# Two-block transformer kernel: one group of memory values and one modulation row change places, and token-major groups wait chunk by chunk

## The reference

```python
# first block, for each of 2 layers
h = layer_norm(ALPHA * h + 0.5 * swiglu(h, ffn1_gate[l], ffn1_up[l], ffn1_down[l]), ...)
z = h @ w_in[l]                      # split into the inputs of three mixers
mix = concat([y_conv, y_rec, y_pool]) @ w_out[l]
h = layer_norm(ALPHA * h + mix, ...)
h = layer_norm(ALPHA * h + cross_attn(h, mem, ca_q[l], ca_k[l], ca_v[l], ca_o[l]), ...)
h = layer_norm(ALPHA * h + 0.5 * swiglu(h, ffn2_gate[l], ffn2_up[l], ffn2_down[l]), ...)

def cross_attn(x, mem, wq, wk, wv, wo):   # 4 heads of 256
    q, k, v = x @ wq, mem @ wk, mem @ wv  # 256 memory rows
    ... softmax(q k^T) v, then @ wo

# second block: attention and an expert layer in each of 2 layers,
# shifted and scaled by rows that depend on a condition c alone
mod = silu(c) @ ada_w[i] + ada_b[i]       # 6 x 1024 per layer; the same for c_ctx
w = softmax(top scores) * gelu(u_tab[expert] . h)   # 128 rows gathered per token
out = sum over the 128 of w * v_tab[expert]
```

## Time and profile before

| | us |
|---|---|
| timed runs, median of 3 (lowest, highest) | 3248.68 (3248.24, 3252.84) |
| the profiled execution, device time | 3234.46 |
| its span from first to last instruction | 3232.2 |
| TensorE busy | 3055.6 (95%) |
| VectorE busy | 2133.4 (66%) |
| ScalarE busy | 952.0 (29%) |
| GpSimd busy | 1226.2 (38%) |

### The profile page before, as it was taken

One profiled execution on the slowest core, in us unless ns is written; L12 is line 12 of the kernel. 1 busy time (PEld: TensorE's weight loads), 2 busy tenths in 40 slices (PEclk: granted clock), 3 DMA queues, 4 the chain that ended last, 5 costly groups with the idle time before them and its releaser, 6 DMA issues.

```text
span 3232.2 us, 39640 instructions
## 1 busy us (share of the span) xinstructions
PE 3055.6 (95%) x13179; PEld 2183.1 (68%) x13185; DVE 2133.4 (66%) x4328; ACT 952.0 (29%) x2504; POOL 1226.2 (38%) x1136
## 2 busy tenths in 40 slices
PE   9999999999999999999999999989888999987777
PEld 7688888888888888887885845535335855532224
DVE  7877889756555457766455695667555596577444
ACT  2320012211001002121003464335455464343333
POOL 1003545344435443343430254434443144444332
PEclk9999999999999999999999999999999999999999
DMA  9787989798998997788988899999999899999998
GB/s 363 256 288 281 373 352 350 267 359 330 355 353 347 356 330 272 268 338 344 354 308 294 336 422 419 421 419 421 418 421 378 319 420 420 421 421 421 421 421 352
DMA packets 252469, 1164.47 MB, mean 360 GB/s; under 512 B 27304, under 2 KB 34952, under 8 KB 186400
## 3 DMA queue, kind: packets, MB, share of 16 engines
q0 software_dynamic: 153792, 828.44, 63.6%
q1 hardware_dynamic: 98480, 334.10, 28.5%
q10 hardware_dynamic: 48, 0.05, 0.0%
HBM read 1161.39 MB, written 1.10 MB: 360 GB/s over the span
## 4 chain that ended last, share of the span: by engine, by line
PE 32%; DMA 16%; DVE 5%; ACT 4%; issue 1%; POOL 0%; ACTq 0%; SPq 0%; POOLq 0%; DVEq 0%
DMA ring<-in_peer_uv,idx 12%; PE ps_a L1471 12%; PE ps_b L1529 5%; DMA arena<-in_peer_uv,idx 3%; PE ps_a L1537 2%; DVE ring L2962 2%; ACT arena L1762 2%; PE ps_a L774 1%; PE ps_b L1292 1%; PE ps_b L1237 1%; PE ps_b L787 1%; ACT L1762 1%; PE ps_a L1292 1%; PE ps_b L1028 1%; ACT wts L1762 1%
## 5 line engine op out<-in xcount | busy, mean ns | idle before, releaser
L1471 PE MATMUL ps_a<-ring,arena 128*128 128x512 f32 x1728 | 819.4, 608 | 129.1 <-ACT arena L1762 128.6
L749 POOL DMA_INDIRECT ring<-in_peer_uv,idx x448 | 494.8, 1104 | 879.0 <-PE ps_a L1471 620.8
L2962 DVE SCALAR_TENSOR_TENSOR ring<-ring,h_tm 128x1024 f32<-128x1024 f32 x448 | 546.7, 1223 | 378.0 <-DMA ring<-in_peer_uv,idx 377.3
L712 POOL DMA_INDIRECT ring<-in_peer_uv,idx_now x512 | 580.7, 1134 | 415.3 <-DVE arena L2780 151.4
L1471 PEld LDWEIGHTS ps_a<-ring,arena 128*128 128x128 f32 x1728 | 308.1, 191 | 561.3 <-ACT arena L1762 293.8
L1529 PE MATMUL ps_b<-x_t,ring 128*128 128x256 f32 x2816 | 623.3, 380 | 0.8 <-DMA ring<-in_ffn 0.5
L1529 PEld LDWEIGHTS ps_b<-x_t,ring 128*128 128x128 f32 x2816 | 533.6, 190 | 79.0 <-ACT x_t L1762 3.5
L1762 ACT ACTIVATE arena<-ps_b 128x256 f32<-128x256 f32 (+3 forms) x218 | 99.3, 457 | 1195.9 <-PE ps_b L1529 827.7
L1537 PE MATMUL ps_a<-arena,ring 128*128 128x256 f32 x1408 | 318.7, 380 | 0.0
L2780 DVE SCALAR_TENSOR_TENSOR arena<-ring,h_tm 128x1024 f32<-128x1024 f32 x256 | 299.1, 1220 | 20.0 <-DMA ring<-in_peer_uv,idx_now 16.6
L1537 PEld LDWEIGHTS ps_a<-arena,ring 128*128 128x128 f32 x1408 | 267.7, 190 | 39.1 <-issue 3.5
(11 more groups left out here) (460 smaller groups left out, 3357.9 us busy)
## 6 DMA issues: line engine op xcount, KB each, us to landing
ring<-in_ffn SPq DMA_DIRECT2D x264, 512.0 KB, 7.0
wring<-in_second_w SPq DMA_DIRECT2D x166, 512.0 KB, 4.8
wring<-in_mix_w SPq DMA_DIRECT2D x120, 512.0 KB, 6.4
ring<-in_ada_rows POOLq DMA_DIRECT2D x44, 512.0 KB, 5.7
ring<-in_second_w SPq DMA_DIRECT2D x12, 1024.0 KB, 10.2
ring<-in_peer_uv,idx_now POOLq DMA_INDIRECT x512, 8.4
ring<-in_peer_uv,idx POOLq DMA_INDIRECT x448, 14.8
arena<-in_second_w SPq DMA_DIRECT2D x13, 512.0 KB, 11.1
```

What stands on the lines that cost most here:

```text
L712: G.indirect_dma_start(rows[:, s, :], None, table, bass.IndirectOffsetOnAxis(ap=idx_now[:, half, s:s + 1], axis=0)).then_inc(rows_in[s], p ...
L749: G.indirect_dma_start(pairs[slot].rearrange("p c d -> p (c d)"), None, a["peer_uv"], bass.IndirectOffsetOnAxis(ap=idx[:, b, s:s + 1], axi ...
L1471: ins = mm(ps_a[:, b * D + j * 512:b * D + (j + 1) * 512], diags[:, at % DIAGS, :], pairs[at % PAIRS][:, 1, j * 512:(j + 1) * 512], start= ...
L2962: V.scalar_tensor_tensor(row, row, 1.0, h_tm[:, n // SLOTS, :], ALU.mult, ALU.mult, accum_out=dots[:, n % SLOTS:n % SLOTS + 1]).then_inc(d ...
```

## The change

Three things.

1. Layer 1's group 13 (chunks 26 and 27 of its `mix_w`, `MOVED` = 26) leaves the mixer. It is computed in layer 0's last norm by `moved_between` into `ps_b[:, 512:1024]` and copied by ScalarE to `moved_v`. The chunks behind it are loaded and counted without it; the groups' banks alternate accordingly.
2. The modulation row that stood in that norm goes to VectorE, as a second row in layer 1's first feed-forward: `mod_row_sums(1, 0, row_acc_2, 1)` behind the first eight slots. TensorE sums it over partitions into `ps_c`, ahead of the other row's product, and ScalarE takes it from there first. SyncE loads this row at the start of the stage, into slots 2, 3, 0, 1; the row that was loaded there is now loaded between the fourth and the fifth turn of the loop. Because of the shifted slots, `value_between` uses slots 2 and 3 in layer 1.
3. `tm_group` runs the chunks outside, over both token blocks, and waits for each chunk when it comes to it; `last_values` also waits for each chunk by itself.

```diff
@@ SyncE
                     if w == 0:
-                        mod_row_loads(row_at)
+                        mod_row_loads(row_at - l, 2 * l)
...
-                    with sp.loop(FT_TURNS, **ff_turn) as i:
+                    looped = FT_TURNS - 1 if (l, w) == (1, 0) else FT_TURNS
+                    with sp.loop(looped, **ff_turn) as i:
...
-                    if w == 0:
+                    if (l, w) == (0, 0):
                         chunk_loads(a["mix_w"], mix_at, MIX_CHUNKS - WR)
+                    elif (l, w) == (1, 0):
+                        mod_row_loads(row_at, 2)
+                        for ft in range(FT_STEP):
+                            for part in range(3):
+                                ff_loads(looped * FT_STEP + (l * (2 * FT) + (w * FT + 2 + ft)), ft, part)
+                        chunk_loads(a["mix_w"], mix_at, 2, 2)
+                        chunk_loads(a["mix_w"], mix_at + 2, MOVED - 2)
+                        chunk_loads(a["mix_w"], mix_at + MOVED + 2, MIX_CHUNKS - WR - MOVED - 2)
+                    elif l == 0:
+                        chunk_loads(a["mix_w"], MIX_CHUNKS + MOVED, 2)
                     else:
                         mod_row_loads(row_at + 3)
@@ TensorE
             def tm_group(c, bank, src):
-                w = [chunk((c + t) % WR) for t in range(2)]
-                for b in range(NB):
-                    for k in range(KT):
-                        ins = mm(bank[:, b * T:(b + 1) * T], src[:, k, b * P:(b + 1) * P],
-                                 w[k // 4][:, (k % 4) * T:(k % 4 + 1) * T], start=k == 0, stop=k == KT - 1)
-                        if b == NB - 1 and k in (3, 7):
-                            ins.then_inc(chunk_done, pe.adds(chunk_done))
+                for t in range(2):
+                    w = chunk((c + t) % WR)
+                    for b in range(NB):
+                        for k in range(4 * t, 4 * t + 4):
+                            ins = mm(bank[:, b * T:(b + 1) * T], src[:, k, b * P:(b + 1) * P],
+                                     w[:, (k % 4) * T:(k % 4 + 1) * T], start=b + k == 0, stop=k == KT - 1,
+                                     skip_group_check=True)
+                    ins.then_inc(chunk_done, pe.adds(chunk_done))
...
                 gate_up(0, True)
                 mod_row_free()
+                if second_row:
+                    eng.wait_ge(z_done, pe.now(z_done))
...
                 eng.wait_ge(chunk_done, pe.now(chunk_done))
+                if second_row:
+                    mm(ps_c[0:2, :], mean_d[:, 0:2], row_acc_2, start=True, stop=True).then_inc(
+                        row_summed, pe.adds(row_summed))
+                    pe.skip(mod_row_taken, 1)
...
                 between(0, 1)
+                if between == value_between and l:
+                    eng.wait_ge(mod_row_taken, pe.now(mod_row_taken, 1))
...
+            def moved_between(i0, i1):
+                if i0 == 0:
+                    mod_row_free()
+                for i in range(i0, i1):
+                    b, k = i // KT, i % KT
                     if b == 0 and k % 4 == 0:
                         chunk(k // 4)
-                    ins = mm(ps_b[:, b * T:(b + 1) * T], mem_t[:, k, b * P:(b + 1) * P],
+                    ins = mm(ps_b[:, 512 + b * T:512 + (b + 1) * T], mem_t[:, k, b * P:(b + 1) * P],
                              wring[:, k // 4, (k % 4) * T:(k % 4 + 1) * T], start=k == 0, stop=k == KT - 1)
...
-                group(13, 26, mem_t, tm=True)
+                if l == 0:
+                    group(13, MOVED, mem_t, tm=True)
...
-                layer_norm(mod_row_between, finish if l == L - 1 else None)
+                layer_norm(mod_row_between if l else moved_between, finish if l == L - 1 else None)
@@ ScalarE
                 feed_forward()
+                if l:
+                    mod_row_take(row_at - 1, SECOND_ROW, mod_row)
                 mod_row_take(row_at, 2, mod_row)
...
-                mod_row_take(row_at + 3, 1, mod_row)
+                if l == 0:
+                    eng.wait_ge(chunk_done, ac.next(chunk_done, 2))
+                    act(moved_v, ps_b[:, 512:1024].rearrange("p (b t) -> p b t", t=T), ACT.Copy).then_inc(
+                        z_done, ac.adds(z_done))
+                else:
+                    mod_row_take(row_at + 3, 1, mod_row)
@@ VectorE
                 hidden_tile(0)
                 some_slots(summing, h, at, HEAD_SLOTS, acc_first)
+                if (l, w) == (1, 0):
+                    mod_row_sums(l, w, row_acc_2, 1)
                 with ve.loop(FT_TURNS, up_done=FT_STEP, silu_done=FT_STEP, down_done=FT_STEP, hidden_done=FT_STEP,
                              **per_turn) as i:
```

More of the change, by code:

```diff
@@ L540, in _, with mod_row_loads @@
             chunk_loads(a["early_w"], 6, 2, 2)
-            def mod_row_loads(i):
-                chunk_loads(a["second_w"], LAYER_1 + WR * ROW_AT[i], WR)
+            def mod_row_loads(i, first=0):
+                chunk_loads(a["second_w"], LAYER_1 + WR * ROW_AT[i], WR, first)
             chunk_loads(a["second_w"], FIRST_ADA, QKV_CHUNKS)
@@ L1589, in value_between @@
                     b, k = i // KT, i % KT
+                    s = k // 4 + 2 * l
+                    if b == 0 and k % 4 == 0:
+                        chunk(s)
+                    ins = mm(ps_b[:, b * T:(b + 1) * T], mem_t[:, k, b * P:(b + 1) * P],
+                             wring[:, s, (k % 4) * T:(k % 4 + 1) * T], start=k == 0, stop=k == KT - 1)
+                    if b == NB - 1 and k % 4 == 3:
+                        ins.then_inc(chunk_done, pe.adds(chunk_done))
+                if i1 == 2 * KT:
+                    pe.skip(z_done, 1)
+            def moved_between(i0, i1):
[3 more added lines that the diff above has]
+                    b, k = i // KT, i % KT
                     if b == 0 and k % 4 == 0:
                         chunk(k // 4)
-                    ins = mm(ps_b[:, b * T:(b + 1) * T], mem_t[:, k, b * P:(b + 1) * P],
+                    ins = mm(ps_b[:, 512 + b * T:512 + (b + 1) * T], mem_t[:, k, b * P:(b + 1) * P],
                              wring[:, k // 4, (k % 4) * T:(k % 4 + 1) * T], start=k == 0, stop=k == KT - 1)
@@ L1623, in group @@
                     eng.wait_ge(z_done, pe.now(z_done, 1))
-                    odd = (g + 1 if g < 12 else g) % 2
+                    odd = (g + 1 if g < 12 or l and g < 18 else g) % 2
                     bank = ps_b[:, odd * 512:(odd + 1) * 512]
+                    if l and c < MOVED:
+                        c += 2
                     if tm:
@@ L1792, in mod_row_take @@
             def mod_row_take(i, bank, row):
-                if bank == 2:
+                if bank in (2, SECOND_ROW):
                     eng.wait_ge(row_summed, ac.next(row_summed))
@@ L2328, in _ @@
                 group(11, z_g[:, 2:4, :], ACT.Sigmoid)
-                group(13, ca_v[:, 1])
+                if l == 0:
+                    group(13, ca_v[:, 1])
                 eng.wait_ge(o_done, ac.next(o_done))
@@ L3166, in later_search, with mod_row_sums @@
                     expert_ids(0, 1, 4, split=True)
-            def mod_row_sums(l, w):
-                loads = ROW_LOADS + l * (MIX_CHUNKS // WR + 4) + w * (MIX_CHUNKS // WR + 2)
+            def mod_row_sums(l, w, row=row_acc, back=0):
+                loads = ROW_LOADS + l * (MIX_CHUNKS // WR + 4) + w * (MIX_CHUNKS // WR + 2) - back
+                first = 2 if (l, w) == (1, 0) else 0
                 for k in range(KT):
-                    part, weight = wring[:, k // 2, k % 2 * 512:(k % 2 + 1) * 512], cond[:, 2 * k:2 * k + 1]
+                    s = (first + k // 2) % WR
+                    part, weight = wring[:, s, k % 2 * 512:(k % 2 + 1) * 512], cond[:, 2 * k:2 * k + 1]
                     if k % 2 == 0:
-                        eng.wait_ge(weights_in[k // 2], 16 * loads)
+                        eng.wait_ge(weights_in[s], 16 * (loads + 1 if s < first else loads))
                     if k == 0:
-                        ins = V.tensor_scalar(row_acc, part, weight, None, ALU.mult)
+                        ins = V.tensor_scalar(row, part, weight, None, ALU.mult)
                     else:
                         eng.wait_ge(row_step, ve.now(row_step))
-                        ins = V.scalar_tensor_tensor(row_acc, part, weight, row_acc, ALU.mult, ALU.add)
+                        ins = V.scalar_tensor_tensor(row, part, weight, row, ALU.mult, ALU.add)
                     if k < KT - 1:
```

39 lines of the change are left out of this document (26 added, 13 removed).

## The result

The changed kernel takes 3256.62 us, the median of 14 runs (3253.44 to 3260.22), the kernel before beside it 3249.89 us (14 runs, 3245.61 to 3252.84). The ratio is 1.0019, 95% interval [1.0012, 1.0027]: 6.7 us slower by the medians. The forecast was 3250.4 us, 1.7 us slower, in a range of 3242 to 3256; the time lies 0.6 us above it.

A forecast was written before the change was run, and what follows sets the result against it. The prediction took TensorE to bound the changed stages, with DMA share 0.93 in the feed-forward. Its terms, -0.5 - 5.5 - 1.6 + 1.1 + 1.0 + 5.5 + 1.7, made +1.7 us: 3250.4 us, range 3242 to 3256.

The forecast's parts named there:

- The norm: Layer 0's last norm, with the moved group as filler instead of the row: 11.05 us long instead of 11.54, -0.5 us.
- The group's removal: Layer 1's mixer: 32 matmuls go, and the products behind them start earlier once VectorE's copies end, -5.5 us.
- chunk by chunk: Token-major groups in both layers: the waits for a chunk go, -1.6 us.
- The third rival: Layer 1's mixer: removing the group gains nothing, as the products wait for something unseen; 3255.9 us, chance 0.05.
- VectorE's second row: Layer 1's first feed-forward: the added sum delays VectorE, so TensorE waits ahead of tile 1's down product, +1.1 us.
- the second sum: Layer 1's first feed-forward: TensorE's additional sum over partitions costs as much as the present one, +1.0 us.
- The wait at tile 18: Layer 1's first feed-forward: gate weights come late behind four row chunks on SyncE's queue, 4.7 to 7.3 us, taken as +5.5.
- the clock: Behind the late gate weights of tile 18: TensorE's granted clock falls to about half for 3.4 us, +1.7 us.
- the lower end: Six transfers ahead of tile 18's gate product, sharing 407 GB/s with 2.08 MB of gathers: 14.7 us, a wait of 4.7.
- The upper end: The same six transfers at tile 18 with half of the bandwidth all along: 17.3 us, a wait of 7.3 us.
- The second rival: At tile 18 SyncE's queue gets a third of the bandwidth: wait 13 to 16 us, 3258 to 3261 us, chance 0.10.
- the first rival: No wait at tile 18, as gathers leave gaps that SyncE's queue fills: -5.5 us, 3243.2 us, chance 0.26.

The follow-up runs named there:

- without the second row: The changed kernel with VectorE's moved row neither loaded nor summed, a constant written in its place: 3228.70 us, ratio 0.9973 to the kernel before.
- both chunks again: The changed kernel with token-major groups and last values waiting for both their chunks first, as before the change: 3256.86 us, ratio 1.0026 to the kernel before.
- half loads: The changed kernel with each of the four late row loads cut from 512 KB to 256 KB: 3237.84 us, ratio 1.0006 to the kernel before.

## Why the prediction was wrong where it was

**The norm, -0.5.** Right: 11.05 us, as forecast.

**The group's removal, -5.5, and chunk by chunk, -1.6.** Right. The products wait 1.20 us for VectorE (forecast about 1.4), and the wait at 505 us is gone. With the norm these three terms are 7.6 us; measured without the second row, 8.4 us [4.9 to 12.3]. The third rival, a removal worth nothing, is out. So is the worry that a later stage might swallow the gain.

**VectorE's second row, +1.1, and the second sum, +1.0.** Nearly right: 0.86 and 0.86 us.

**The wait at tile 18, +5.5, and the clock, +1.7: the step that failed, in size.** The place, the cause and the order on SyncE's queue were right; its length was 7.47, 8.89 and 9.36 us in three executions, the clock's price 2.99, 2.54 and 2.08 us. Together 10.5, 11.4 and 11.4 instead of 7.2. What went wrong is in the choice between the two ends. The lower, 14.7 us from the first issue, put into the sum the 2.08 MB that the gathers move in 10.3 us; but the stretch that counts is the longer one that the queue itself makes. The reason for staying near the lower end was that the gathers pause in part of each period; over this stretch they went on at 177 GB/s, where they had moved 202 in the 10.3 us. The DMA queues from 1157.5 to 1175.5 us in the changed kernel:

```profile
q1 hardware_dynamic: 1027, 3.77, 55.3%
q0 software_dynamic: 872, 3.18, 44.8%
```

3.18 MB of gathers in 18 us, against 2.08 MB in 10.3. With 3.18 in place of 2.08 the prediction's own formula gives 1.9 + (3.15 + 3.18) / 0.407 = 17.5 us, and the measured time from the first issue is 17.7. The upper end, 17.3 us by the even split, was the one to take, and the sum would have been 1.8 us higher in the wait alone. With both chunks again it was 19.1 us, and when the changed kernel ran again 1170.01 - 1150.46 = 19.6 us, so that even this end wasn't a bound. The queues from 1150.1 to 1170 us there:

```profile
q1 hardware_dynamic: 1127, 4.13, 54.3%
q0 software_dynamic: 987, 3.59, 45.3%
```

SyncE's queue gets its half of the bandwidth, and a little more, in both; but it moves 3.77 and 4.13 MB in that time and not the 3.15 MB of the six transfers. The rest isn't left over from before: from 1157.0 to 1158.4 us in the first of the two, and from 1149.0 to 1151.0 in the second, the trace has no packet of this queue. So 0.6 and 1.0 MB of the loads issued behind the gate weights of tile 18 move before these are there, which the prediction left out. That its upper end comes out so near is in part luck, since the share is off the other way. Once all six are issued the queue has more than half, 3.40 of 5.86 MB from 1161 to 1175.5 us:

```profile
q1 hardware_dynamic: 934, 3.40, 59.3%
q0 software_dynamic: 669, 2.46, 42.7%
```

The second rival isn't reached: in its terms, 3.15 MB in the time less 1.9 us, the rate is 199, 183 and 178 GB/s in the three executions, and it decides from 170, a wait of 10.4 us.

The half loads check this by dose: on the same chip they take 1168.41 - 1152.85 = 15.6 us, 4.0 less for 1.05 MB less, or 262 GB/s for what was taken away. The wait falls from 9.36 to 5.37 us, the clock's price from 2.08 to 1.54, together by 4.5; the time against the kernel before by 5.1 - 0.7 = 4.4. So fewer bytes ahead of the weights shorten the wait. How much is due to bytes and how much to the number of transfers isn't shown: these are single executions, and with full loads they range from 17.7 to 19.6 us, so that the dose is worth 2.1 to 4.0 us. The clock's term was sized well for the wait it was made for: 1.7 us forecast behind 5.5, 1.54 measured behind 5.37. Behind the longer waits it was 2.1 to 3.0.

The Trainium skill (DMA: Bandwidth & Descriptors, Anatomy of one DMA — SWDGE (gpsimd) path) fits one transfer as 2.0 us plus its bytes by 436 GB/s; as an estimate that was 9.2 us for the six, and the first rival, no wait at tile 18. The trace has 17.7 and 19.6 us: carried over from one transfer to six beside a second queue that is always loaded, the fit is off by about a factor of two.

**The sum again.** With what was measured: -0.5 - 5.5 - 1.6 + 0.9 + 0.9 + 11.4 = +5.6 us, beside 5.1 (second chip); with 10.5 in place of 11.4 and 0.63 us at tile 4 it is +5.3, beside 6.7 [3.9 to 8.8] (first comparison). What is left over, 0.5 us too much and 1.4 too little, is less than the intervals.

**The point of reference.** The prediction was made on an execution 14 us below the timed runs and carried the difference over unscaled. That was harmless, since the halts are in both kernels. It would not have been for somebody who subtracted the two spans and looked for 21 us.

**The range.** It ended at 3256, since the case of a wait beyond 7.3 us was left to the second rival alone, with 0.10. Between the upper end of the forecast (7.3) and that rival (from 10.4, with 13 to 16 at the third) lay a gap with nothing in it, and there all three waits are; the longest, 9.36, is also over the 9 us that the prediction named as a sign of its being wrong. That the time misses the range by only 0.6 us, less than its interval, doesn't make the step right: its two terms together were 3.3 us short in the first comparison and 4.2 us in the two other executions.

## What to carry to other kernels

When transfers are moved in a queue, count the bytes between the last load that comes in time and the first that is needed, and set against them half of the full rate for the whole of the stretch that comes out, not the other queue's traffic in the short stretch of before. Here that gave 17.3 us of 17.7 to 19.6, so add something for the loads behind. What can be loaded where the DMA engines have room, here at the start of the stage, should be there: the same 2.1 MB made TensorE wait 7.5 to 9.4 us ahead of tile 18 and at most 0.3 us when they were loaded first. And before a wait is put into the program of the engine that issues the loads, look at what stands behind it.

## What the runs showed of the hardware that was not expected

- One program has two levels of time by chip: 3248.3 and 3236.6 us for the kernel before. On the first chip, and in the profile of the changed kernel from the first comparison, TensorE halts for 2 to 4 us without a recorded cause, at the same instructions of the two attention stages in both kernels (L1758 and L788 of the changed one, L1715 and L774 of the one before), and the matmuls behind it run slower. On the second chip no profile shows them. The same place in the changed kernel, in the first comparison and on the second chip (12 matmuls each):

```profile
699.06 4.40 PE L788 MATMUL ps_a<-arena,wring 128*128 128x256 f32 x12 [3.10 <-issue]
```
```profile
694.61 2.76 PE L788 MATMUL ps_a<-arena,wring 128*128 128x256 f32 x12
```

All that the trace has beside them is full DMA engines, and on the second chip these are as full in the same place (422 GB/s from 696 to 699 us). A late load of the program's own instructions comes to mind, but the trace lists packets of such loads (q8, q14), and none lies in the two halts: in the changed kernel's first profile the nearest are at 680 and 703 us. It wasn't tried and stays open.
- The two queues share about evenly even where one of them carries what TensorE is waiting for: 3.77 of 6.95 MB and 4.13 of 7.72 MB went to SyncE's. But the six transfers in question got only 3.15 MB of it, 178 GB/s from the first issue in one execution and 161 in the other, where the engines moved 386 to 388.
- The price of the slow clock isn't proportional to the wait: 1.54 us behind 5.37, 2.99 behind 7.47, 2.54 behind 8.89, 2.08 behind 9.36, one execution each.
